# Another order of the steps in a software-pipelined neighbourhood attention

## The chip, the cores and the metric

The kernel runs as one program on one core of a Trainium2 chip. The core has a matrix engine (PE, with its weight loads shown apart as PEld), a vector engine (DVE), a scalar engine (ACT), a general engine (POOL) and a queue engine (SP). Each runs its own list of instructions strictly in program order and waits on semaphores that the others raise. The metric is the device time of one execution in microseconds. All arithmetic here is in 32-bit floats.

## The reference, cut to what matters

Two transformer-like blocks run one after the other on 512 tokens of width 1024: attention, state-space scan and experts, then a second mixer and experts. The change lies in one stage of the first block, the neighbourhood attention: 16 heads of width 64 on a grid of 8 rows by 64 columns, with 256 further context keys.

```python
s_loc = jnp.einsum('bqhd,bkhd->bhqk', q_r, k_r).astype(jnp.float32) * scale + bias
s_loc = jnp.where(mask, s_loc, -jnp.inf)
s_ctx = jnp.einsum('bqhd,bkhd->bhqk', q_r, k_ctx).astype(jnp.float32) * scale
p = jax.nn.softmax(jnp.concatenate([s_loc, s_ctx], axis=-1), axis=-1).astype(v.dtype)
return (jnp.einsum('bhqk,bkhd->bqhd', p[..., :n_loc], v_r)
        + jnp.einsum('bhqk,bkhd->bqhd', p[..., n_loc:], v_ctx))
```

## The kernel before, in words

The stage works in 32 units, numbered u = 0 to 31. A unit is one pair of heads (8 pairs) and one tile of 128 queries (4 tiles). A unit has 256 local keys and 256 context keys, so a score row has 512 entries for each of its two heads. The scores are computed with their sign turned, so the softmax looks for a minimum and the exponential has scale -1.

Each unit passes through seven steps on three engines. The letters are used in the prediction:

- S(u), `scores` on PE (L935, L938): the scores of both heads, into `na_score`. It waits until W(u-2) has read the same half of the score buffer (`exped`).
- H(u), `highest` on DVE (L1003, L1007): a reduction over the context scores, then for each head the local scores with their bias added and reduced, and a small read of the accumulator. It waits for S(u) (`scored`).
- W(u), `weights` on ACT (L982): for each head the exponential of 512 entries into `na_p`, and a small read of the sum. It waits for H(u), head by head (`topped`).
- N(u), `normalise` on DVE (L1013, L1015): the reciprocal of the sums, and two multiplications over 512 entries. It waits for W(u), both heads (`exped`).
- T(u), `turn` on PE (L947): eight 128x128 transposes of `na_p` into `na_flip`. It waits for N(u) (`normed`) and for C(u-1).
- C(u), the copy on ACT (L991): `na_flip` to `na_pT`. It waits for T(u) and for V(u-2).
- V(u), `values` on PE (L961), and take(u), a copy on DVE (L1020): the product with the values, and its move to its place. V(u) waits for C(u) and take(u-2); take(u) waits for V(u).

The buffers for scores, `na_p`, `na_pT` and the output each have two halves, used by turns (u % 2); `na_flip` has one. The order on each engine is written out by hand. In the loop over u, PE runs S(u+2), T(u), V(u-1); DVE runs N(u), take(u-2), H(u+2); ACT runs C(u), W(u+2). Ahead of the loop PE has S(0), S(1); DVE has H(0), H(1); ACT has W(0), W(1). During the first dozen units POOL builds the bias tables for the following heads (L905 to L920). The stage stands between two barriers: the next stage starts when every engine has finished.

Of the kernel before, what the change touches and what calls it, by code (L numbers as in the profile page):

```python
# [290 lines left out]
class RowNorm:  # L291
# [102 lines left out]
    def turn(self, pe, after=None):  # L394
        if self.branch is not None:
            pe.wait_ge(self.diag_ready, 1)
            for h in range(2):
                last = pe.matmul(self.spread[:, h, :], self.k.const("ones"), self.diag[:, 4 * h:4 * h + 4, :].rearrange("p j n -> p (j n)"),
                                 start=True, stop=True)
            last.then_inc(self.spread_ready, 1)  # L400
        for t in range(LT):
            pe.wait_ge(self.row_ready, t + 1)
            for h in range(2):
                if t >= 2:
                    pe.wait_ge(self.second_taken if h else self.first_taken, t - 1)
                for j in range(4):
                    last = pe.transpose(self.source(t, h)[:, j, :], self.xn[:, t, (4 * h + j) * P:(4 * h + j + 1) * P], self.k.const("ident"))
                last.then_inc(self.tile_ready, 1)
            if after is not None and t:
                self.wait_tile(pe, t - 1)  # L410
                after(t - 1)
        if after is not None:
            self.wait_tile(pe, LT - 1)
            after(LT - 1)
# [451 lines left out]
def neighbourhood_attention(k, q, key, kc, v, vc, base, inputs_loaded):  # L866
# [4 lines left out]
    units = [(pair, i) for pair in range(HEADS // 2) for i in range(LT)]  # L871
# [3 lines left out]
    with ctx:  # L875
# [13 lines left out]
        def table(h, i):  # L889
            if TILE_TABLE[i] == 1:  # L890
                return base[:, h].rearrange("p s n -> p (s n)")
            return edge[:, h, TILE_TABLE[i] // 2].rearrange("p s n -> p (s n)")

        @block.gpsimd
        def _(pool):
            S = WIN_W // 2

            def tile(x, heads, s):
                return x[:, heads, s].rearrange("p h (r c) -> p h r c", c=WIN_W)

            def off(t, cols):
                return mask[:, t, cols].unsqueeze(1).unsqueeze(1).to_broadcast([P, BIAS_HEADS, GRID_H, cols.stop - cols.start])

            near, far, whole = slice(0, S), slice(S, WIN_W), slice(0, WIN_W)
            pool.memset(edge[:, :, 0, 0, :], -NEG).then_inc(blank, 1)  # L905
            pool.memset(edge[:, :, 1, 0, :], -NEG).then_inc(blank, 1)
            pool.wait_ge(blank, 2)
            for loaded in inputs_loaded:
                pool.wait_ge(loaded, 16)
            for n in range(HEADS // BIAS_HEADS):  # L910
                heads = slice(n * BIAS_HEADS, (n + 1) * BIAS_HEADS)
                left, right = edge[:, :, 0], edge[:, :, 1]
                before, after = tile(base, heads, 0), tile(base, heads, 1)
                pool.tensor_tensor(tile(left, heads, 0)[:, :, :, near], off(0, near), before[:, :, :, far], ALU.subtract).then_inc(edged, 1)
                pool.tensor_tensor(tile(left, heads, 1), off(1, whole), after, ALU.subtract).then_inc(edged, 1)
                pool.tensor_tensor(tile(right, heads, 0)[:, :, :, far], off(4, far), after[:, :, :, near], ALU.subtract).then_inc(edged, 1)
                pool.tensor_tensor(tile(right, heads, 1), off(5, whole), before, ALU.subtract).then_inc(edged, 1)
                pool.wait_ge(edged, 4 * (n + 1))
                pool.tensor_tensor(before, off(2, whole), before, ALU.subtract).then_inc(tabled, 1)
                pool.tensor_tensor(after, off(3, whole), after, ALU.subtract).then_inc(tabled, 1)  # L920

        @block.tensor
        def _(pe):
            def scores(u):
                pair, i = units[u]
                b = u % 2
                if u >= 2:
                    pe.wait_ge(exped, 2 * (u - 1))
                for n in range(3):
                    for hp in range(2):  # L930
                        d = slice(hp * HD, (hp + 1) * HD)
                        queries = q[d, pair, i * P:(i + 1) * P]
                        if n < 2:
                            t = TILE_KEYS[i][n]
                            last = pe.matmul(score[:, b, hp, n * P:(n + 1) * P], queries, key[d, pair, t * P:(t + 1) * P],  # L935
                                             start=True, stop=True)
                        else:
                            last = pe.matmul(score[:, b, hp, N_LOC:N_KEY], queries, kc[d, pair, :], start=True, stop=True)  # L938
                last.then_inc(scored, 1)

            def turn(u):
                pe.wait_ge(normed, 2 * (u + 1))
                if u:
                    pe.wait_ge(flip_taken, u)
                for hp in range(2):
                    for j in range(KB):
                        last = pe.transpose(flip[:, hp, j * P:(j + 1) * P], p[:, u % 2, hp, j * P:(j + 1) * P], k.const("ident"))  # L947
                last.then_inc(flipped, 1)

            def values(u):  # L950
                pair, i = units[u]
                b = u % 2
                pe.wait_ge(flip_taken, u + 1)
                if u >= 2:
                    pe.wait_ge(taken, u - 1)
                for j in range(KB):
                    for hp in range(2):
                        d = slice(hp * HD, (hp + 1) * HD)
                        cols = slice((2 * pair + hp) * HD, (2 * pair + hp + 1) * HD)
                        rows = v[:, TILE_KEYS[i][j], cols] if j < 2 else vc[:, j - 2, cols]  # L960
                        last = pe.matmul(out[d, b, 0:P], rows, pT[:, b, hp, j * P:(j + 1) * P], start=(j == 0), stop=(j == KB - 1))  # L961
                last.then_inc(valued, 1)

            scores(0)
            scores(1)
            for u in range(len(units)):
                if u + 2 < len(units):
                    scores(u + 2)
                turn(u)
                if u:  # L970
                    values(u - 1)
            values(len(units) - 1)

        @block.scalar
        def _(act):
# [19 lines left out]
        @block.vector  # L995
        def _(dve):
            link = Steps(dve, dve_step)

            def highest(u):
                pair, i = units[u]  # L1000
                b = u % 2
                dve.wait_ge(scored, u + 1)
                link(dve.tensor_reduce(low[:, b, :], score[:, b, :, N_LOC:N_KEY], AX.X, ALU.min))  # L1003
                for hp in range(2):
                    h = 2 * pair + hp
                    dve.wait_ge(tabled, 2 * (h // BIAS_HEADS + 1))
                    dve.tensor_tensor_reduce(score[:, b, hp, 0:N_LOC], score[:, b, hp, 0:N_LOC], table(h, i), 1.0, low[:, b, hp:hp + 1],  # L1007
                                             ALU.add, ALU.min, top[:, b, hp:hp + 1]).then_inc(topped, 1)

            def normalise(u):  # L1010
                b = u % 2
                dve.wait_ge(exped, 2 * (u + 1))
                link(dve.reciprocal(inv[:, b, :], total[:, b, :]))  # L1013
                for hp in range(2):
                    dve.tensor_scalar(p[:, b, hp, :], p[:, b, hp, :], inv[:, b, hp:hp + 1], None, ALU.mult).then_inc(normed, 1)  # L1015

            def take(u):
                pair, i = units[u]
                dve.wait_ge(valued, u + 1)
                dve.tensor_copy(q[:, pair, i * P:(i + 1) * P], out[:, u % 2, 0:P]).then_inc(taken, 1)  # L1020

            highest(0)
            highest(1)
            for u in range(len(units)):
                normalise(u)
                if u >= 2:
                    take(u - 2)
                if u + 2 < len(units):
                    highest(u + 2)
            take(len(units) - 2)  # L1030
            take(len(units) - 1)
            dve.wait_ge(taken, len(units))

# [2942 lines left out]
```

## Time and profile before

| | us |
|---|---|
| median of three runs | 3514.05 |
| the three runs | 3511.38, 3514.05, 3514.18 |
| the profiled execution, its own time | 3511.38 |
| its span in the trace | 3509.6 |
| PE busy over the span | 3147.2 (90%) |
| DVE busy over the span | 1085.1 (31%) |
| ACT busy over the span | 561.2 (16%) |
| the stage, first score matmul to end of the last copy out | 312.2 to 430.2 |

The span is what the trace covers; 1.8 us of the execution lie around it. The stage is about 3.4% of it. A busy share over the whole span says little of this stage, so the rows below are taken inside it. Matmuls overlap in PE's pipeline; the start of one group to the start of the next is a better measure of what it costs than its own duration.

### The profile page before, as it was taken

What the parts mean: (1) busy time and instruction counts of PE and PEld (TensorE: products, weight loads), DVE (VectorE), ACT (ScalarE), POOL (GpSimd) and SP (SyncE); (2) the same over time, 40 slices, a digit from 0 to 9 for tenths busy, and PEclk for the clock granted to TensorE, in tenths of its full rate; (3) what the DMA queues carried; (4) which work ended last, traced back from release to release, by engine and by line L of the source; (5) the groups of instructions that cost most, each with busy time, mean ns of one, the idle gap of its engine ahead of it and who ended that gap; (6) DMA issues with size and microseconds to landing.
All of it is one profiled execution on the core that took longest, in us unless ns stands there. A gap on an engine that the chain in (4) does not pass through costs nothing. (4 is left out here: it accounts for less than half of the span.)

```text
span 3509.6 us, 38152 instructions
## 1 busy us (share of the span) xinstructions
PE 3147.2 (90%) x15886; PEld 1658.7 (47%) x15886; DVE 1085.1 (31%) x2141; ACT 561.2 (16%) x1184; POOL 287.8 (8%) x270
## 2 busy tenths in 40 slices
PE   6998999997989999898999999997997889997986
PEld 5444744663654444744344434433545763644332
DVE  2233703553672201410111011103146653522113
ACT  2002601111652100200000000002012321301111
POOL 0003000005741000000000000000001200001001
PEclk9999999996999999799999999999998889997997
DMA  7621011100002221489999999996310021053996
GB/s 270 247 91 48 18 60 48 48 25 24 1 1 72 96 72 48 193 338 428 428 428 427 428 427 425 428 428 280 131 36 2 3 98 63 13 222 129 410 425 263
DMA packets 131937, 668.56 MB, mean 190 GB/s; under 512 B 17627, under 2 KB 45694, under 8 KB 98745
## 3 DMA queue, kind: packets, MB, share of 16 engines
q1 hardware_dynamic: 115385, 630.24, 44.4%
q10 hardware_dynamic: 11344, 27.79, 2.1%
q0 software_dynamic: 5040, 8.13, 0.7%
q8 instruction: 125, 2.05, 0.2%
q14 instruction: 43, 0.35, 0.0%
HBM read 672.15 MB, written 14.16 MB: 196 GB/s over the span
## 5 line engine op out<-in xcount | busy, mean ns | idle before, releaser
L2014 PE MATMUL ec_wide<-ec_ring,ec_xg 128*64 128x512 f32 x2048 | 459.7, 603 | 18.0 <-issue 13.8
L2014 PEld LDWEIGHTS ec_wide<-ec_ring,ec_xg 128*64 128x64 f32 x2048 | 147.9, 139 | 309.5 <-issue 305.3
L2048 PE MATMUL ec_acc<-ec_ring,ec_hidT 128*64 128x512 f32 x1024 | 233.5, 611 | 29.2 <-DMA ec_ring<-in_w_exp_down 28.4
L2173 DVE TENSOR_SCALAR ec_xg<-ec_piece,ordered 128x128 f32<-128x128 f32 x64 | 21.9, 404 | 570.7 <-PE ec_piece L2062 570.7
L2048 PEld LDWEIGHTS ec_acc<-ec_ring,ec_hidT 128*64 128x64 f32 x1024 | 81.8, 141 | 178.0 <-issue 177.7
L2062 PEld LDWEIGHTS ec_piece<-ec_sel,x 128*128 128x128 f32 x512 | 122.9, 336 | 8.6 <-issue 5.7
L2062 PE MATMUL ec_piece<-ec_sel,x 128*128 128x128 f32 x512 | 124.4, 405 | 2.8 <-DVE ec_sel L2155 2.8
L3713 PE MATMUL hm_gu<-hm_ring,hm_xg 128*64 128x512 f32 x432 | 118.8, 616 | 5.9 <-DMA hm_ring<-in_moe_w_gu 3.2
L2755 POOL TENSOR_TENSOR solve_T<-const_rw,solve_T 128x512 f32<-128x512 f32 x8 | 10.1, 1267 | 1304.7 <-DVE solve_T L2793 1304.7
L2137 ACT ACTIVATE ec_hidT<-ec_acc 128x512 f32<-128x512 f32 x32 | 17.4, 594 | 518.9 <-PE ec_acc L2037 518.9
L1152 PE MATMUL conv_main<-hT,conv_early 128*128 128x512 f32 x192 | 86.2, 604 | 2.9 <-DVE bcT L1234 2.9
L567 PE MATMUL p_rkv_acc<-ahead_rkv,h2mT 128*128 128x384 f32 x256 | 84.6, 494 | 1.9 <-DVEq L575 1.9
L1152 PE MATMUL conv_main<-hT,conv_late 128*128 128x512 f32 x192 | 84.4, 592 | 0.0
L1406 ACT ACTIVATE ssd_seg_in<-const_all,a 128x128 f32<-128x128 f32 x256 | 77.8, 390 | 0.5 <-PEq L1090 0.5
L2188 DVE TENSOR_TENSOR branch<-branch,ec_piece 128x512 f32<-128x512 f32 x64 | 44.0, 688 | 105.5 <-PE ec_piece L2080 105.5
L1366 PE MATMUL ssd_seg<-ssd_seg_in,const_all 128*128 128x512 f32 x128 | 62.9, 615 | 10.0 <-DVE ssd_cbm L1428 10.0
L2080 PE MATMUL ec_piece<-ec_y,ec_selT 128*128 128x512 f32 x128 | 63.8, 622 | 7.3 <-DVE ec_selT L2182 6.1
L567 PEld LDWEIGHTS p_rkv_acc<-ahead_rkv,h2mT 128*128 128x128 f32 x256 | 49.5, 194 | 36.8 <-DVEq L575 2.3
L3713 PEld LDWEIGHTS hm_gu<-hm_ring,hm_xg 128*64 128x64 f32 x432 | 37.8, 142 | 57.5 <-issue 54.5
L1392 PE MATMUL ssd_yd<-ssd_xd,ssd_lx 128*128 128x64 f32 x512 | 61.2, 273 | 2.1 <-DVE ssd_lx L1432 2.1
L1392 PEld LDWEIGHTS ssd_yd<-ssd_xd,ssd_lx 128*128 128x128 f32 x512 | 60.0, 193 | 3.0 <-DVE ssd_lx L1432 3.0
L567 PE MATMUL na_br_g_acc<-hT,ahead_na 128*128 128x512 f32 x128 | 56.6, 605 | 5.2 <-ACTq L575 5.2
(652 smaller groups left out, 5038.7 us busy)
## 6 DMA issues: line engine op xcount, KB each, us to landing
ec_ring<-in_w_exp_gate SPq DMA_DIRECT2D x64, 2048.0 KB, 17.7
ec_ring<-in_w_exp_up SPq DMA_DIRECT2D x64, 2048.0 KB, 27.0
ec_ring<-in_w_exp_down SPq DMA_DIRECT2D x64, 2048.0 KB, 19.5
hm_ring<-in_moe_w_gu SPq DMA_DIRECT2D x27, 2048.0 KB, 24.9
hm_ring<-in_moe_w_down SPq DMA_DIRECT2D x11, 2048.0 KB, 29.2
ahead_qkv<-in_w_in SPq DMA_DIRECT2D x10, 2048.0 KB, 9.9
hm_ring_late<-in_moe_w_down SPq DMA_DIRECT2D x5, 2048.0 KB, 25.3
u2T<-in_moe_w_gu SPq DMA_DIRECT2D x5, 2048.0 KB, 23.3
```

The costliest lines, as they stand in the source:

```text
L567: last = pe.matmul(acc[0:rows, bank, 0:cols], stat(j), mov(j), start=(j == 0), stop=(j == kt - 1))
L1152: last = pe.matmul(main[:, i % 2, :], w[:, j, m * P:(m + 1) * P], hT[:, j, :], start=(j == 0), stop=(j == KD - 1))
L1366: pe.matmul(seg[:, h, :], k.const("after" if d == 0 else "before"), seg_in[:, m % 2, 4 * h:4 * h + 4].rearrange("p h l -> p (h l)"), start ...
L1392: last = pe.matmul(yd[:, m % 2, h * 64:(h + 1) * 64], lx[:, m % 2, h, :], xd[:, n % 2, h * 64:(h + 1) * 64], start=True, stop=True)
L1406: ins = act.activation(seg_in[:, m % 2, h, :], cum, ACT.Copy, scale=a[:, tile(units[mains[m]]), col:col + 1])
L2014: last = pe.matmul(wide[half(e), b, :], xg[:, u % 2, j, half(e)], w[e][:, a, b * 512:(b + 1) * 512], start=(j == 0), stop=(j == KD - 1))
L2048: last = pe.matmul(acc[half(e), h, :], hidT[:, f, half(e)], w[e][:, r, h * 512:(h + 1) * 512], start=(f == 0), stop=(f == FT - 1))
L2062: last = pe.matmul(piece[:, m % 2, i * P:(i + 1) * P], x[:, t, HALF * h + i::KD], sel[:, t, :], start=(t == 0), stop=(t == LT - 1))
L2080: pe.matmul(piece[:, m % 2, :], selT[:, t * P:(t + 1) * P], y[:, h * 512:(h + 1) * 512], start=True, stop=True).then_inc(piece_done, 1)
L2173: last = dve.tensor_scalar(xg[:, u % 2, j, :], piece[:, m % 2, i * P:(i + 1) * P], scale_cols[:, j:j + 1], shift_cols[:, j:j + 1], ALU.mul ...
L2188: dve.tensor_tensor(place, place, piece[:, m % 2, :], ALU.add).then_inc(piece_taken, 1)
L3713: last = pe.matmul(gu[half(e), u % 2, :], xg[:, u % 2, j, half(e)], w[e][:, j, :], start=(j == 0), stop=(j == KD - 1))
```

## The change

On PE the loop's order becomes T(u), S(u+2), V(u) in place of S(u+2), T(u), V(u-1), and the last V behind the loop goes. On DVE N(0) moves ahead of the loop, and the loop's order becomes N(u+1), take(u-1), H(u+2) in place of N(u), take(u-2), H(u+2). ACT's order, the instructions, their sizes, the buffers and every wait's condition are the same.

```diff
@@ -964,12 +964,10 @@
             scores(0)
             scores(1)
             for u in range(len(units)):
+                turn(u)
                 if u + 2 < len(units):
                     scores(u + 2)
-                turn(u)
-                if u:
-                    values(u - 1)
-            values(len(units) - 1)
+                values(u)
 
@@ -1021,13 +1019,14 @@
 
             highest(0)
             highest(1)
+            normalise(0)
             for u in range(len(units)):
-                normalise(u)
-                if u >= 2:
-                    take(u - 2)
+                if u + 1 < len(units):
+                    normalise(u + 1)
+                if u:
+                    take(u - 1)
                 if u + 2 < len(units):
                     highest(u + 2)
-            take(len(units) - 2)
             take(len(units) - 1)
             dve.wait_ge(taken, len(units))
```

The order on DVE before, from N(0) on. RECIPROCAL and TENSOR_SCALAR are N, TENSOR_REDUCE and the ISA rows are H, COPY is take. The rows are N(0), H(2), and N(1).

```order
L1013 RECIPROCAL na_inv<-na_total 128x2
L1015 TENSOR_SCALAR na_p<-na_p,na_inv 128x512 x2
L1003 TENSOR_REDUCE na_low<-na_score 128x2
L1007 ISA na_score,na_top<-na_score,na_base,na_low 128x256
L1007 ISA na_top 128x1
L1007 ISA na_score,na_top<-na_score,na_base,na_low 128x256
L1007 ISA na_top 128x1
L1013 RECIPROCAL na_inv<-na_total 128x2
L1015 TENSOR_SCALAR na_p<-na_p,na_inv 128x512 x2
```

The same place after the change: N(0), N(1), H(2), then N(2), take(0) and the start of H(3). Line numbers are two lower.

```order
L1011 RECIPROCAL na_inv<-na_total 128x2
L1013 TENSOR_SCALAR na_p<-na_p,na_inv 128x512 x2
L1011 RECIPROCAL na_inv<-na_total 128x2
L1013 TENSOR_SCALAR na_p<-na_p,na_inv 128x512 x2
L1001 TENSOR_REDUCE na_low<-na_score 128x2
L1005 ISA na_score,na_top<-na_score,na_base,na_low 128x256
L1005 ISA na_top 128x1
L1005 ISA na_score,na_top<-na_score,na_base,na_low 128x256
L1005 ISA na_top 128x1
L1011 RECIPROCAL na_inv<-na_total 128x2
L1013 TENSOR_SCALAR na_p<-na_p,na_inv 128x512 x2
L1018 COPY q<-na_out 128x128
```

N(u+1) now stands directly ahead of H(u+2), where N(u) stood; the copy out of a unit comes one unit earlier.

The order on PE before, from T(0) on: T(0), S(3), T(1), V(0). The `na_flip` row is T, the two `na_score` rows are S, the two `na_out` rows are V.

```order
L947 MATMUL na_flip<-const_all,na_p 128x128 x8
L935 MATMUL na_score<-key,q 128x128 x4
L938 MATMUL na_score<-kc,q 128x256 x2
L947 MATMUL na_flip<-const_all,na_p 128x128 x8
L961 MATMUL na_out<-na_pT,v 64x128 x4
L961 MATMUL na_out<-na_pT,vc 64x128 x4
```

After it, from T(0) on: T(0), S(2), V(0), T(1).

```order
L947 MATMUL na_flip<-const_all,na_p 128x128 x8
L935 MATMUL na_score<-key,q 128x128 x4
L938 MATMUL na_score<-kc,q 128x256 x2
L961 MATMUL na_out<-na_pT,v 64x128 x4
L961 MATMUL na_out<-na_pT,vc 64x128 x4
L947 MATMUL na_flip<-const_all,na_p 128x128 x8
```

S(2), which stood ahead of T(0), now stands behind it, and V follows the transposes of its own unit with only S between them.

## Rows read from the trace of the kernel before

**Rows 1.** Windows; busy us per engine (instructions), then granted clock, DMA share, GB/s.

```profile
core 0: us, PE busy (x) PEld busy (x) DVE busy (x) ACT busy (x) POOL busy (x), PEclk, DMA share, GB/s
...
353.00:373.00 20.00, 20.00 (x232) 15.81 (x232) 17.69 (x58) 14.65 (x33) 0.00 (x0) 1.00 0.01 2
```

**Rows 2.** Timeline of one settled unit: start, duration, engine, line, [idle before <-releaser].

```profile
374.63 0.86 PEld L947 LDWEIGHTS na_flip<-const_all,na_p 128*128 128x128 f32 x8 [0.33 <-DVE na_p L1015]
...
374.75 0.69 DVE L1003 TENSOR_REDUCE na_low<-na_score 128x2 f32<-128x512 f32 x1 [0.30 <-PE na_score L938]
...
375.65 0.66 PE L961 MATMUL na_out<-na_pT,v 128*64 128x128 f32 x8
375.76 1.02 ACT L991 ACTIVATE na_pT<-na_flip 128x1024 f32<-128x1024 f32 x1 [0.77 <-PE na_flip L947]
375.88 0.14 DVE L1007 DVE_READ_ACCUMULATOR2_ANT na_top<- 128x1 f32 x1
...
376.29 0.16 DVE L1013 RECIPROCAL na_inv<-na_total 128x2 f32<-128x2 f32 x1
376.49 0.88 DVE L1015 TENSOR_SCALAR na_p<-na_p,na_inv 128x512 f32<-128x512 f32 x2
...
376.68 0.72 PE L935 MATMUL na_score<-key,q 64*128 64x128 f32 x8
376.68 0.68 ACT L982 ACTIVATE na_p<-na_score,na_top 128x512 f32<-128x512 f32 x1
...
377.29 0.28 DVE L1020 COPY q<-na_out 128x128 f32<-128x128 f32 x1
...
377.76 1.09 PE L947 MATMUL na_flip<-const_all,na_p 128*128 128x128 f32 x8
...
377.92 0.21 ACT L982 ACTIVATION_READ_ACCUMULATOR na_p<-na_score,na_top 128x1 f32 x1
```

**Rows 3.** Timeline, the last units of the stage.

```profile
424.81 0.21 ACT L982 ACTIVATION_READ_ACCUMULATOR na_p<-na_score,na_top 128x1 f32 x1
425.05 0.17 DVE L1013 RECIPROCAL na_inv<-na_total 128x2 f32<-128x2 f32 x1 [0.58 <-ACT na_p L982]
425.25 0.88 DVE L1015 TENSOR_SCALAR na_p<-na_p,na_inv 128x512 f32<-128x512 f32 x2
...
426.63 1.07 PE L947 MATMUL na_flip<-const_all,na_p 128*128 128x128 f32 x8 [0.19 <-ACT na_pT L991]
...
429.95 0.29 DVE L1020 COPY q<-na_out 128x128 f32<-128x128 f32 x1 [0.89 <-PE na_out L961]
```

**Rows 4.** Timeline, the first units of the stage.

```profile
324.87 2.76 DVE L1015 TENSOR_SCALAR na_p<-na_p,na_inv 128x512 f32<-128x512 f32 x2
...
327.54 0.68 DVE L1003 TENSOR_REDUCE na_low<-na_score 128x2 f32<-128x512 f32 x1
...
327.68 1.97 PE L947 MATMUL na_flip<-const_all,na_p 128*128 128x128 f32 x8 [1.20 <-DVE na_p L1015]
...
329.58 1.23 PE L935 MATMUL na_score<-key,q 64*128 64x128 f32 x8
...
331.70 0.69 DVE L1003 TENSOR_REDUCE na_low<-na_score 128x2 f32<-128x512 f32 x1 [0.55 <-PE na_score L938]
331.84 0.21 ACT L982 ACTIVATION_READ_ACCUMULATOR na_p<-na_score,na_top 128x1 f32 x1
...
335.93 0.28 DVE L1020 COPY q<-na_out 128x128 f32<-128x128 f32 x1
...
336.13 0.68 DVE L1003 TENSOR_REDUCE na_low<-na_score 128x2 f32<-128x512 f32 x1
```

**Rows 5.** Timeline, the last multiplication of `na_p` beside POOL's table work.

```profile
342.03 1.19 DVE L1015 TENSOR_SCALAR na_p<-na_p,na_inv 128x512 f32<-128x512 f32 x2
```

**Rows 6.** Windows in the first part of the stage, columns as in Rows 1.

```profile
328.00:330.00 2.00, 2.00 (x12) 1.67 (x12) 1.92 (x8) 0.32 (x1) 2.00 (x3) 0.50 0.00 0
...
334.00:342.00 8.00, 5.97 (x70) 4.67 (x72) 7.87 (x18) 4.31 (x10) 7.92 (x8) 1.00 0.00 0
```

## The prediction

> **What bounds the kernel now.** I read three views in this order: the windows over the settled part of the stage, the timeline of one unit in it, and the timelines at the stage's two ends. The letters S, H, W, N, T, C, V and take are the steps of a unit as the text on the kernel names them.
>
> The windows show PE busy for 20.00 of 20 us at clock 1.00, DVE for 17.69 and ACT for 14.65 [rows 1]. PE is full; the other two have room. The timeline of a unit agrees. T starts at 374.63 and the next T at 377.76, so a unit takes 3.13 us, and it consists of T to V (374.63 to 375.65, 1.02), V to S (to 376.68, 1.03) and S to T (to 377.76, 1.08) with nothing between [rows 2]. The row of T's weight load names DVE as its releaser with 0.33 us of idle time, but DVE's multiplication has long ended (in the next unit 376.49 + 0.88 = 377.37, T at 377.76) [rows 2]. So that wait is not the bound: PE goes from S's matmuls to the transposes there, and its queue sets the pace. DVE's only idle time is 0.30 us, for S [rows 2].
>
> How much slack do the other steps have? W starts at 376.68 and its last read ends at 377.92 + 0.21 = 378.13 [rows 2]. The N that uses these sums starts a whole unit after the one at 376.29, thus at 376.29 + 3.13 = 379.42, because DVE's order puts H(u+3) ahead of N(u+2). So N finds its sums ready 1.29 us before it wants them. That slack comes from the order alone, and it is what the change spends.
>
> **The ring that the change closes.** After it, DVE runs N(u+1), take(u-1), H(u+2). N(u+1) needs W(u+1); H(u+2) stands behind N(u+1) on DVE; W(u+2) needs H(u+2). So one turn of W to N to H to W advances one unit. Before, DVE ran N(u), then H(u+2), and the same turn (W(u), N(u), H(u+2), W(u+2)) advanced two units. The length of a turn, from rows:
> - W's sums ready to N's start: 424.81 + 0.21 = 425.02 to 425.05, 0.03 [rows 3].
> - Reciprocal to multiplication: 425.05 to 425.25, 0.20 [rows 3].
> - Multiplication pair to take: 376.49 to 377.29, 0.80 [rows 2].
> - take to the start of H: 335.93 to 336.13, 0.20, in the one place where H does not wait for S [rows 4].
> - H to the first head's minimum: 374.75 to 375.88 + 0.14 = 376.02, 1.27 [rows 2].
> - That minimum to W: 0.03, taken equal to the first term.
> - W, both heads: 376.68 to 378.13, 1.45 [rows 2]. The second head's minimum is no later than its exponential needs it.
>
> The sum is 3.98 us a unit. Before, two units shared it: 1.99 each, well under PE's 3.13. After, each unit pays it, and it exceeds PE's 3.13.
>
> Does anything else lie in the ring? Put zero where W(u+1) ends. C(u) takes ACT until 1.0 (1.02 [rows 2]), and W(u+2) starts only at 2.53, so ACT has room. V(u) runs from 1.05 to 2.1, T(u+1) to 3.1 (N(u+1) is done at 1.1), and C(u+1) wants it at 3.98. S(u+3) runs to 4.2, and H(u+3) wants it at 3.98 + 1.23 = 5.2. So PE has 0.9 us to spare at T and 1.0 at S. Those are what would be late next. take(u-1) is long ready. The unknown is whether the seven terms keep their size when they stand back to back. The lower end is PE's 3.13, no loss at all. For the upper end, take not overlapped (0.28 for 0.20) and 0.10 more on H and W give 4.2. I take 3.98, since each term is a row.
>
> **The PE part.** T(u), S(u+2), V(u): the same 22 matmuls a unit, so nothing is removed. C(u) (1.02) now lies behind S(u+2) (1.08) alone, so V is covered almost exactly. Its price inside the ring is nothing. If PE were still the bound it would gain at most the 0.33 of idle time less the 0.17 that a usual switch shows, 0.16 a unit, by no longer going straight from S to T; it could lose about as much if V waits for C. Both are hidden by the 0.9 us of idle time.
>
> **The start.** T(0) waits for N(0), whose multiplications end at 324.87 + 2.76 = 327.63, and starts at 327.68 as before [rows 4]. S(2) used to be done by then, and H(2) started at 327.54 [rows 4]. Now S(2) is behind T(0). At the slow clock (0.50 of 2.4 GHz, so 1.2 GHz, in 328 to 330 [rows 6]) T takes 327.68 to 329.58, and S 329.58 to its reader at 331.70 [rows 4]. So H(2) starts at 331.70, and W(2) ends at 331.70 + 1.27 + 0.03 + 1.45 = 334.45, where it ended at 331.84 + 0.21 = 332.05 [rows 4]. N(1), moved ahead of H(2), fits before 331.70 even at 2.76.
>
> While POOL builds tables, the multiplication pair takes up to 2.76 in place of 0.88, and 1.19 at the end of that work [rows 4, 5]. N(2) and N(3) still fall in it. I charge 1.45 and 1.0, with bounds 0 and 1.9 each. W(3) ends at 334.45 + 3.98 + 1.45 = 339.9, W(4) at 344.9. W(5) to W(31) are 27 turns, 107.5 us: W(31) ends at 452.4. Before it ended at 425.02 [rows 3].
>
> **The end.** C(30) follows W(31) on ACT and takes until 453.4; V(30) until 454.5; then T(31) to the last copy takes what it took, 426.63 to 429.95 + 0.29 = 430.24, 3.61 us [rows 3]. The stage ends at 458.1.
>
> **The sum.** 458.1 - 430.24 = 27.9 us: settled turns 27 x (3.98 - 3.13) = 23.0, start and end 4.9. What follows is behind a barrier and shifts with it. On the profiled execution's own 3511.38 that gives 3539.3. That run was the fastest of three, 2.7 under the median, on which the sum gives 3542. I forecast 3541, near the median.
>
> **Rivals.**
> *A, the clock drops.* PE would be idle about 0.9 of 4 us a unit. At the slow clock T and S take 1.90 and 2.07 [rows 4], V by the same ratio 2.0: 6.0 us a unit, more than the ring. For every unit from the third that is 29 x (6.0 - 3.98) = 59 more, 3600. Against it: in 334 to 342 PE was busy 5.97 of 8 us, in unit-long bursts with gaps, and the clock stayed 1.00 [rows 6]; and once slow, PE is full again, after which it rose in this very stage. Half the units slow is more likely than all: 3570.
> The Trainium skill, "TensorE: Matmul & The Clock Gate", section "Part 4: PE-mode transpose", says transposes do not count as activity for this clock; then about half of each turn would count and rival A would gain. The settled stretch, a third of it transposes, ran at 1.00, which does not decide it, and the rule stays inside A's chance.
>
> *B, the other side: not slower.* If W's sums reached N before DVE asks for them, the ring would not bind, and PE's order would. This decides at a turn below 3.13. Then PE saves up to 0.16 on 31 units, 5 us, less the start's 2.4: 3511. For it: that DVE is only 17.69 of 20 busy and N has 1.29 of slack. Against it: the slack is in the order, and the seven terms leave no 0.85 to find.
>
> *C, the ring is there but longer.* Port contention between DVE and ACT or a later S gives 4.2 a unit: 29 x 0.22 = 6 more, 3547. The rows of a full unit already have all three engines at work, so this is inside my own range.
>
> **How the numbers follow.** My forecast, with C as its upper part, 0.86: 3533 to 3551, from ring terms 0.15 off either way (4 us), the start's 3 and the baseline's 2. A 0.08, B 0.06. For 8 in 10 I take 3531 to 3554. A measurement of this kernel tells about 0.2% (7 us) from no change. B's 0.06 is 0.02 faster by more than that and 0.04 within it, since its 3511 is itself within that of the median. All else is slower, 0.94.
>
> **What would show it.** Right: T to T near 4.0 us; the reciprocal's row with idle time released by ACT in each unit; PE idle 0.8 to 0.9 us a unit, released by C or N; DVE's wait for S gone; H(2) near 331.7; the stage ending near 458; clock 1.00. Wrong: T to T at 3.1 (B), or PEclk of 0.5 to 0.8 after 334 (A).

## The result and the profile after

The changed kernel took 3540.32 us (median of 3 runs, 3538.31 to 3540.56), the kernel before 3514.05. The ratio is 1.0076, with a 95% interval of 1.0052 to 1.0098: slower, by 0.8%. The forecast was 3541 in a range of 3531 to 3554. The profiled execution has a span of 3538.1 us, where before it was 3509.6.

| the stage, from POOL's first instruction to the end of the last copy out | start | end | us |
|---|---|---|---|
| before | 312.17 | 430.24 | 118.1 |
| after | 313.29 | 461.44 | 148.2 |

So the stage grew by 30.1 us. It started 1.1 us later in this execution, ahead of anything that was changed, so times of the two are compared less that amount. The span grew by 28.5 only: 2.7 us of the 31.2 at the stage's end are made up in later stages, where the two programs are alike. The lag behind the kernel before is 31.3 us at 873.9 us of that kernel's trace, 30.0 at 1052.0 and 28.7 at 2458.3, so it is lost in two places at least. Its cause stays open; it is of the size by which the runs of the kernel before differ (3511.38 to 3514.18).

The windows of the settled part, columns as in [rows 1]:

```profile
353.00:373.00 20.00, 16.09 (x183) 12.39 (x182) 14.11 (x48) 11.80 (x25) 0.00 (x0) 1.00 0.00 1
```

PE, which was busy for all 20.00 us [rows 1], is now busy for 16.09; DVE went from 17.69 to 14.11, ACT from 14.65 to 11.80. All three have idle time. That is how a ring of waits (a closed turn, in which each step waits for the one before it and the last releases the first) looks in a table of busy shares: no engine is full, and none of the shares names a culprit. The clock is 1.00 as before.

One turn in the timeline of the changed kernel, to be put beside [rows 2] (lines of DVE and ACT are two lower):

```profile
382.26 0.20 ACT L980 ACTIVATION_READ_ACCUMULATOR na_p<-na_score,na_top 128x1 f32 x1
...
382.50 0.17 DVE L1011 RECIPROCAL na_inv<-na_total 128x2 f32<-128x2 f32 x1 [1.11 <-ACT na_p L980]
382.70 0.88 DVE L1013 TENSOR_SCALAR na_p<-na_p,na_inv 128x512 f32<-128x512 f32 x2
...
383.43 0.66 PE L961 MATMUL na_out<-na_pT,v 128*64 128x128 f32 x8 [0.78 <-ACT na_pT L989]
383.50 0.28 DVE L1018 COPY q<-na_out 128x128 f32<-128x128 f32 x1
383.69 0.68 DVE L1001 TENSOR_REDUCE na_low<-na_score 128x2 f32<-128x512 f32 x1
...
384.45 1.09 PE L947 MATMUL na_flip<-const_all,na_p 128*128 128x128 f32 x8
384.82 0.14 DVE L1005 DVE_READ_ACCUMULATOR2_ANT na_top<- 128x1 f32 x1
...
385.00 0.69 ACT L980 ACTIVATE na_p<-na_score,na_top 128x512 f32<-128x512 f32 x1 [1.62 <-DVE na_top L1005]
...
386.24 0.20 ACT L980 ACTIVATION_READ_ACCUMULATOR na_p<-na_score,na_top 128x1 f32 x1
...
388.43 1.09 PE L947 MATMUL na_flip<-const_all,na_p 128*128 128x128 f32 x8
```

T to T is 388.43 - 384.45 = 3.98 us. Follow the turn: W's sums are ready at 382.46, N starts at 382.50 after 1.11 us of waiting for them, the copy at 383.50, H at 383.69, its first minimum is ready at 384.96, W starts at 385.00 after 1.62 us of waiting for it, and ends at 386.44. Each of DVE and ACT waits for the other in every unit. H's wait for S, 0.30 us a unit in [rows 2], is gone.

### The profile page after: what moved, and what is told of

It is laid out like the page before. It is cut to its first block and busy times, and to the rows that moved or that the text cites. A ratio compares the mean times of both kernels' runs of the same rounds, so it can differ in the third digit from the quotient of the medians.

```text
span 3538.1 us, 38152 instructions
## 1 busy us (share of the span) xinstructions
PE 3149.4 (89%) x15886; PEld 1661.1 (47%) x15886; DVE 1086.8 (31%) x2141; ACT 560.8 (16%) x1184; POOL 287.0 (8%) x270
```

## The experiments

Each run's ratio is to the kernel before, measured on the same chip (3510.72 us, 15 runs, for the first four; 3512.28, 19 runs, for the last two). The changed kernel was not run again beside them, and its interval overlaps those of the first and the third experiment, so how these two differ from it is read from the traces. The theory: the turn W, N, H, W on ACT and DVE now advances one unit in place of two, and its 3.98 us set the pace. The main rival came from the list of waits of the changed kernel:

```profile
ACT na_p L980 <- DVE na_top L1005: 50.1, 29, 3.7
PEld na_out L961 <- ACT na_pT L989: 36.2, 30, 2.1
DVE na_inv L1011 <- ACT na_p L980: 33.2, 30, 1.1
```

The columns are total us, times, longest. The second line is new and looks like the cause: V stands right behind C of its own unit, and PE waits there in every unit.

**Only the DVE part.** In the changed kernel PE's loop got its old order back:

```diff
-                turn(u)
                 if u + 2 < len(units):
                     scores(u + 2)
-                values(u)
+                turn(u)
+                if u:
+                    values(u - 1)
+            values(len(units) - 1)
```

> Only DVE's new order (N(u+1), take(u-1), H(u+2)); PE keeps S(u+2), T(u), V(u-1). Ring theory (W, N, H, W once a unit, all on DVE and ACT): T to T stays at 3.98 us, V no longer waits for C, and the stage is some 3 us shorter than with both parts, because S(2) is again ahead of T(0) (1.8 us) and the end is shorter: about 3538 us, 1.007 of the kernel before. Rival (the loss is V's wait for C behind T and S, 36 us in the list of waits of the changed kernel): with V(u-1) the wait and the loss are gone, T to T 3.13, about 3514 us.

Measured: 3534.88 us, 1.0066 (1.0051 to 1.0082). V now has no wait, and the turn is the same to the hundredth:

```profile
380.12 1.09 PE L947 MATMUL na_flip<-const_all,na_p 128*128 128x128 f32 x8
...
382.96 0.17 DVE L1013 RECIPROCAL na_inv<-na_total 128x2 f32<-128x2 f32 x1 [1.11 <-ACT na_p L982]
382.98 0.52 PEld L935 LDWEIGHTS na_score<-key,q 64*128 64x128 f32 x8 [0.98 <-ACT na_p L982]
...
384.10 1.09 PE L947 MATMUL na_flip<-const_all,na_p 128*128 128x128 f32 x8
...
385.12 0.42 PEld L961 LDWEIGHTS na_out<-na_pT,v 128*64 128x64 f32 x8 [0.17 <-issue]
```

PE's idle time only moved, from V to S, which now waits for ACT: 0.98 us in the row of the weight load and 0.74 in that of the matmul, where V's had 0.78. The rival falls: PE's wait for C was an effect. The stage takes 144.4 us (312.33 to 456.75), 3.7 less than with both parts; I had expected some 3.

**Only the PE part.** In the kernel before, PE's loop got the new order, and DVE kept its own:

```diff
-                if u + 2 < len(units):
-                    scores(u + 2)
                 turn(u)
-                if u:
-                    values(u - 1)
-            values(len(units) - 1)
+                if u + 2 < len(units):
+                    scores(u + 2)
+                values(u)
```

> Only PE's new order (T(u), S(u+2), V(u)); DVE keeps N(u), take(u-2), H(u+2). Ring theory: the DVE/ACT ring again spans two units and doesn't bind, but another closes once a unit through PE: N 0.20 + 0.88 + 0.03, T 1.03, S to the reduction's start 1.19, H 1.54, together 4.87 us a unit, 54 us more than before: about 3568 us, 1.0155. Rival 1 (PE's new order costs nothing by itself, all of the loss is the DVE part): 3.13 a unit, about 3516 us. Rival 2 (the PE part is the whole loss): about 3540 us, 3.98 a unit.

Measured: 3568.17 us, 1.0164 (1.0148 to 1.0179). One unit in its timeline:

```profile
379.95 1.09 PE L947 MATMUL na_flip<-const_all,na_p 128*128 128x128 f32 x8 [1.60 <-DVE na_p L1013]
380.98 0.72 PE L935 MATMUL na_score<-key,q 64*128 64x128 f32 x8
...
382.17 0.69 DVE L1001 TENSOR_REDUCE na_low<-na_score 128x2 f32<-128x512 f32 x1 [2.08 <-PE na_score L938]
...
383.72 0.16 DVE L1011 RECIPROCAL na_inv<-na_total 128x2 f32<-128x2 f32 x1
...
384.86 1.09 PE L947 MATMUL na_flip<-const_all,na_p 128*128 128x128 f32 x8 [1.60 <-DVE na_p L1013]
```

T to T is 4.91 us, where 4.87 was expected. Another turn closes here, between DVE and PE: N, T, S, H, and on DVE the next N. So the two parts do not add up. Alone they cost some 24 and 57 us by the medians, together 26: on top of PE's new order, advancing N on DVE takes the turn through PE off the pace and puts the shorter one through ACT in its place. By the two orders, H(u+2) then stands ahead of N(u+2) and no longer of N(u+1), so the turn through PE advances two units, some 2.5 us each. Both rivals in the expectation fall, the one that takes the PE part as free and the one that makes it the whole loss.

**The copy behind H.** In the changed kernel, on DVE:

```diff
-                if u:
-                    take(u - 1)
                 if u + 2 < len(units):
                     highest(u + 2)
+                if u:
+                    take(u - 1)
```

> The changed kernel with one edit: on DVE take(u-1) stands behind H(u+2) in place of ahead of it, so the order is N(u+1), H(u+2), take(u-1). Nothing is removed. Ring theory: the copy's 0.20 us leaves the ring and falls into DVE's idle time: T to T 3.78, 29 turns x 0.20 = 5.8 us less than the changed kernel: about 3534.5 us, 1.0058 of the kernel before. Rival (PE's wait for C or anything outside DVE's order sets the pace): 3.98 a unit and 3540 us, unchanged.

Measured: 3530.74 us, 1.0058 (1.0044 to 1.0071). No work is gone, but the copy is out of the turn:

```profile
381.26 1.09 PE L947 MATMUL na_flip<-const_all,na_p 128*128 128x128 f32 x8
...
381.84 0.28 DVE L1018 COPY q<-na_out 128x128 f32<-128x128 f32 x1
...
383.09 0.17 DVE L1011 RECIPROCAL na_inv<-na_total 128x2 f32<-128x2 f32 x1 [0.97 <-ACT na_p L980]
...
385.05 1.09 PE L947 MATMUL na_flip<-const_all,na_p 128*128 128x128 f32 x8
```

T to T is 3.79 where 3.78 was expected. The stage takes 139.7 us (313.29 to 453.00), 8.4 less than the changed kernel's: 5.7 are the turns, 1.7 the end, whose T(31) here ran at the full clock (below), and 1.0 the multiplications of N(3) beside POOL's table work, which took 1.90 us here and 2.94 in the changed kernel (their row is shown below).

**V between S and T.** In the kernel before, PE's order became S(u+2), V(u-1), T(u):

```diff
                     scores(u + 2)
-                turn(u)
                 if u:
                     values(u - 1)
+                turn(u)
```

> The kernel before with PE's order S(u+2), V(u-1), T(u) in place of S(u+2), T(u), V(u-1); DVE as before. PE is the bound there, so only the switch between kinds of matmul could change: from S to T it takes 1.08 us where the others take 1.02 to 1.03. If the surcharge belongs to that pair: 3.08 a unit, 1.5 us less, about 3512.5 us. If it belongs to S itself: 3.13 and 3514 us. Rival: V(u-1) waits for C(u-1), which has only S(u+2) ahead of it, and the unit gets 0.1 longer: about 3517 us.

Measured: 3515.05 us, 1.0009 (1.0000 to 1.0018). The lower end of the interval is at no change at all, so the trace decides. In it the rival came true: a unit takes 3.23 us, and V waits for C.

```profile
380.69 1.09 PE L947 MATMUL na_flip<-const_all,na_p 128*128 128x128 f32 x8
...
382.89 0.42 PEld L961 LDWEIGHTS na_out<-na_pT,v 128*64 128x64 f32 x8 [0.43 <-ACT na_pT L991]
...
383.92 1.10 PE L947 MATMUL na_flip<-const_all,na_p 128*128 128x128 f32 x8
```

This is what it costs to have only S between T and V where nothing else binds: 0.10 us a unit, since S covers C almost but not quite. In the changed kernel it was hidden, as the prediction had it.

**The wide product first.** In the kernel before, inside S:

```diff
-                for n in range(3):
+                for n in (2, 0, 1):
```

> The kernel before, with one edit inside S: its context product (256 columns a head) comes first and the two local ones (128 columns) last. This settles what e4_v_between left open, since V's wait for C hid it there: S to T takes 1.08 us, T to V and V to S 1.02 to 1.03. If the surcharge comes from the wide product standing last in front of T: 3.08 a unit, 1.5 us less over the stage, too little for the timed runs and plain in the trace. If it belongs to S as a whole: 3.13 as before.

Measured: 3511.66 us, 0.9999 (0.9990 to 1.0008).

```profile
380.17 1.09 PE L947 MATMUL na_flip<-const_all,na_p 128*128 128x128 f32 x8
...
381.68 0.61 PE L961 MATMUL na_out<-na_pT,vc 128*64 128x128 f32 x8
...
382.21 0.70 PE L938 MATMUL na_score<-kc,q 64*128 64x256 f32 x4
...
382.75 0.61 PE L935 MATMUL na_score<-key,q 64*128 64x128 f32 x8
...
383.29 0.86 PEld L947 LDWEIGHTS na_flip<-const_all,na_p 128*128 128x128 f32 x8
383.29 1.09 PE L947 MATMUL na_flip<-const_all,na_p 128*128 128x128 f32 x8
```

S to T still takes 1.08 us and the unit 3.12, so the place of the wide product is not the reason. Nor is it the switch to T: the last part of S takes 0.54 us (382.75 to 383.29), the last part of V before S 0.53 (381.68 to 382.21). The surcharge belongs to S. The idle time in front of T's weight load, 0.33 in [rows 2], is gone from the row, and no time with it: it was weight-load idle time beside busy matmuls, never a loss. The prediction had counted it as something to gain.

**The start of the stage.** A different place, which the timelines of all kernels pointed to: DVE and PE wait there for the first bias tables. In the kernel before:

```diff
-BIAS_HEADS = 4
+BIAS_HEADS = 2
...
-            pool.memset(edge[:, :, 1, 0, :], -NEG).then_inc(blank, 1)
...
+            dve.memset(edge[:, :, 1, 0, :], -NEG).then_inc(blank, 1)
             highest(0)
             highest(1)
```

> The kernel before, with the start of the stage changed: POOL builds the bias tables for two heads at a time in place of four, and DVE fills one of the two blank parts in its idle time. In the kernel before and in the changed one DVE waits 8.2 us for the first tables, with PE idle. PE-bound theory of the settled part: that part keeps 3.13 us a unit, and the first minimum is found sooner by the half of six table steps (7.0 us of them, so 3.5) and the 1.8 us of the blank part: 4 to 5 us off the stage, about 3509.5 us on a median of 3514. Rival: the time is given back by slower multiplications beside POOL (1.2 to 2.8 us a pair in place of 0.9) or by a later wait for a table: under 1 us gained.

Measured: 3504.12 us, 0.9976 (0.9966 to 0.9985): faster than both kernels, by 8.2 us of median against the kernel before. The stage takes 111.3 us (312.79 to 424.1), 6.8 less.

In the kernel before, the wait for the first tables is this:

```profile
322.31 0.49 DVE L1007 CUSTOM_DVE_ANT_0 na_score<-na_score,na_edge,na_low 128x256 f32<-128x256 f32 x1 [8.23 <-POOL na_base L920]
```

And with the change:

```profile
313.29 1.76 DVE L1021 MEMSET na_edge<- 128x2048 f32 x1 [2.31 <-PEq L491]
...
318.99 0.49 DVE L1006 CUSTOM_DVE_ANT_0 na_score<-na_score,na_edge,na_low 128x256 f32<-128x256 f32 x1 [3.35 <-POOL na_base L919]
...
321.54 1.42 DVE L1014 TENSOR_SCALAR na_p<-na_p,na_inv 128x512 f32<-128x512 f32 x2
```

The wait for the tables is 3.35 us in place of 8.23. DVE's own blank part delays its first reduction by 1.0 us, so the first minimum comes 3.9 us sooner. The first multiplication pair took 1.42 beside POOL's shorter steps, where it took 2.76 in [rows 4], and the pairs of N(0) to N(4) together 7.4 where they took 10.7. The work of POOL lasts longer here, until N(7), and that gives back 0.5. So the stage's 6.8 us are 3.9 + 3.4 - 0.5: the give-back that the rival feared went the other way. The two edits were not run apart. The median gained 1.4 us more than this stage did in the one profiled execution; that part stays open.

## Why the prediction was right

The mechanism that the prediction names is the one that the runs show. That its number, 3541, lies within 1 us of the median is in part luck: the stage grew by 30.1 us where 27.9 were forecast, and later stages made up 2.7 of them for no reason that the prediction knew.

Step by step, times of the changed kernel less the 1.1 us (1.12) by which its stage started later:

- **PE is the bound before; N has slack from the order alone.** Right. The DVE order alone, with PE's work and order untouched, turned 3.13 into 3.98 a unit.
- **The turn of 3.98 us.** Right in sum and in each term, which are now 0.04, 0.20, 0.80, 0.19, 1.27, 0.04 and 1.44. The seven terms kept their size when they stood back to back. The last W ends at 454.12 and the fifth unit's at 346.63, both as the trace has them: 27 turns of 3.98. Taking one term of 0.20 out took 0.19 off the period.
- **C, V, T and S have room.** Right: V's 0.78 us of idle time in each unit is room, as the first experiment showed.
- **The PE part.** Right that it is hidden in the ring. Wrong in what it would do if PE were the bound: 0.16 us a unit to gain, or about as much to lose. The 0.33 us of idle time was nothing to gain (3.12 us a unit without it), and PE's order alone closed a turn of 4.91 us, which the prediction did not look for. The price of rival B rests on that gain.
- **The start.** Nearly right. H(2) began at 331.7 as worked out. N(2) and N(3) cost 1.1 and 2.1 extra beside POOL, 3.1 together where I had charged 2.45. W(4) ended at 345.5, forecast 344.9. This is the pair of N(3):

```profile
340.83 2.94 DVE L1013 TENSOR_SCALAR na_p<-na_p,na_inv 128x512 f32<-128x512 f32 x2
```

  POOL's table work ended at 343.5 in the changed kernel, during N(3), and at 342.5 in the kernel before, during N(4): it lies beside the first four or five units, and not the first dozen.
- **The end.** Mis-sized. From T(31) to the last copy I took 3.61 us over from before; it took 5.33:

```profile
456.11 1.90 PE L947 MATMUL na_flip<-const_all,na_p 128*128 128x128 f32 x8
```

  The granted clock had fallen to 0.50 (1.2 GHz) there. The stage ended at 460.3, forecast 458.1. Of these 2.2 us, 1.7 are this and 0.5 what the start and the turns had added.
- **Rival A, the clock.** It did not decide, yet it was not absent. The sign named for it, a clock of 0.5 to 0.8 after 334, appeared for about 3.4 us. Besides the end the clock fell once more near the start, in the windows of the changed kernel:

```profile
343.00:344.00 1.00, 0.17 (x1) 0.18 (x2) 1.00 (x3) 0.00 (x0) 0.49 (x1) 0.80 0.00 0
344.00:345.00 1.00, 1.00 (x6) 1.00 (x7) 0.96 (x2) 0.00 (x0) 0.00 (x0) 0.50 0.00 0
...
347.00:348.00 1.00, 0.87 (x12) 0.47 (x12) 1.00 (x4) 0.55 (x1) 0.00 (x0) 1.00 0.00 0
```

  PE had idled 1.60 us before V(2) and 1.17 for the multiplications of N(3). T(3) and most of S(5) ran slow, and this cost nothing, because S had its 1.0 us to spare. As argued, PE was full at the low clock (1.00 of 1.00 us), and the clock rose again. In the settled part it stayed at 1.00.
- **Rivals B and C.** Neither came true: the ring binds, and at its own length.

## What to carry to other kernels

In a software pipeline over engines with fixed orders, list the closed turns of waits and queue positions, and divide each one's length by the number of units it advances. A step moved one unit earlier or later on one engine changes that divisor, and a turn that was far from binding at half its length can bind at the whole. The waits of the profile then point at every engine in the turn and at bystanders too; which is which is told by moving one step out of the turn and seeing whether the period drops by its length.

## What the runs showed of the hardware that was not expected

The clock's behaviour does not follow from the idle share alone. With only the PE part changed, PE was busy for two thirds of the time and idle for 1.60 us before each T, yet the granted clock stayed 1.00:

```profile
353.00:373.00 20.00, 13.46 (x156) 10.22 (x154) 11.40 (x37) 9.89 (x20) 0.00 (x0) 1.00 0.00 1
...
413.00:473.00 60.00, 39.19 (x432) 29.48 (x432) 34.15 (x114) 30.86 (x64) 0.00 (x0) 1.00 0.00 1
```

In the first units of that same run it had fallen to 0.50 in 338 to 340 and to 0.52 in 344 to 346, after PE had idled 2.58 and 2.13 us for the multiplications. In the changed kernel and with only the DVE part, which are busier, it fell within 0.2 us of the start of T(31), after idle times of 1.86 us, while with the copy behind H, where the longest such wait near the end was 1.66 us, T(31) ran in 1.09. What sets the moment stays open; one execution of each does not settle it. The rule weighed in the prediction, that transposes do not count as activity (the Trainium skill, "TensorE: Matmul & The Clock Gate", "Part 4: PE-mode transpose"), would have made the low clock likelier in these stretches, a third of whose PE work is transposes; it stayed high in all the settled ones, so the runs give the rule no support here, though the other two thirds can explain that too.

The multiplication pair of `na_p` takes 0.88 us alone. Beside table steps of POOL that are up to 512 wide it takes 1.19 to 2.94, beside those of up to 256 (the last experiment) 1.11 to 1.79; for N(0) it is 2.76 against 1.42. The Trainium skill, "SBUF — State Buffer", section "SBUF: two separate sides", describes a port pair for which DVE and GpSimd compete and which one instruction holds until its end; if this pair of operations needs that port pair, shorter instructions on one side mean shorter waits on the other. The rows agree with that, though no run took POOL's work away from a settled unit.
